# Experts in units of 32 rows in column groups, with whole fp32 weights in a ring, instead of blocks of 128 rows with split weights

## What is computed

```
lg   = v @ w_rg + b_rg                      # 4 groups of experts; the best group is taken
le   = v @ w_re + b_re                      # 8 experts in each group; the best 2 of the group
eid  = g_sel * 8 + top_i                    # 2 experts for each of 1032 rows: 2064 assignments
def expert_block(xb, e):                    # 32 experts, D = 1024, FF = 512
    hb = silu(xb @ w_gate[e]) * (xb @ w_up[e])     # 1024 -> 512, twice
    return hb @ w_down[e]                          # 512 -> 1024
f    = sum over the 2 experts of gate * expert_block(v)
y    = layer_norm(alpha * x1 + mod * f)
```

## Time and profile before

| | us |
|---|---|
| median of three runs | 1721.53 |
| the profiled execution | 1723.17 |
| its span, first to last instruction | 1721.5 |
| TensorE busy in the span | 1551.1 (90%) |
| VectorE, ScalarE, GpSimd busy | 1286.8, 798.7, 336.8 |
| moved by DMA | 365.95 MB, mean 213 GB/s |
| mean granted clock of TensorE | 0.947 of 2.4 GHz |

### The profile page before, as it was taken

One profiled execution on the slowest core, in us unless ns is written; L12 is line 12 of the kernel. 1 busy time (PEld: TensorE's weight loads), 2 busy tenths in 40 slices (PEclk: granted clock), 3 DMA queues, 4 the chain that ended last, 5 costly groups with the idle time before them and its releaser, 6 DMA issues.

```text
span 1721.5 us, 24475 instructions
## 1 busy us (share of the span) xinstructions
PE 1551.1 (90%) x8473; PEld 1310.2 (76%) x8473; DVE 1286.8 (75%) x1405; ACT 798.7 (46%) x689; POOL 336.8 (20%) x292
## 2 busy tenths in 40 slices
PE   5799999979999968999955899999999999999873
PEld 4788989978988956858844788888888888888630
DVE  5755647569998878767656778758978788699749
ACT  3322224255556655312220656457756565677510
POOL 4000002110000000000002233323434334344200
PEclk8999999989999988999965999999999999999986
DMA  9566227343333447332232769479978697899662
GB/s 295 189 227 234 65 78 236 123 140 120 105 112 126 136 158 244 110 99 88 65 145 103 303 235 376 175 304 364 376 281 324 246 376 273 331 353 369 266 241 109
DMA packets 135703, 365.95 MB, mean 213 GB/s; under 512 B 19120, under 2 KB 97968, under 8 KB 120152
## 3 DMA queue, kind: packets, MB, share of 16 engines
q1 hardware_dynamic: 113608, 308.19, 49.5%
q0 software_dynamic: 21456, 54.80, 9.1%
q10 hardware_dynamic: 576, 2.10, 0.4%
HBM read 333.07 MB, written 54.90 MB: 225 GB/s over the span
## 4 chain that ended last, share of the span: by engine, by line
PE 53%; DVE 4%; issue 2%; SPq 2%; DMA 1%; ACT 0%; POOL 0%; POOLq 0%; DVEq 0%; ACTq 0%
PE PS L2083 24%; PE PS L2116 13%; PE PS L1966 9%; PE PS L2076 2%; PE PS L2149 1%; PE PS L2105 1%; PE PS L1997 1%; PE PS L2032 1%; SPq L1597 1%; PE PS L1989 1%; DVE st L2489 0%; SPq L1602 0%; DVE lower L2480 0%; DVE arena L2497 0%; DVE arena L2485 0%
## 5 line engine op out<-in xcount | busy, mean ns | idle before, releaser
L2083 PE MATMUL PS<-big 128*128 128x512 f32 x1824 | 435.4, 395 | 8.4 <-DVE big L2425 5.1
L881 PE MATMUL PS<-big 128*128 128x352 f32 x2592 | 435.8, 328 | 1.6 <-DVE big L1135 1.6
L881 PEld LDWEIGHTS PS<-big 128*128 128x128 f32 x2592 | 424.4, 191 | 10.4 <-issue 6.7
L2083 PEld LDWEIGHTS PS<-big 128*128 128x128 f32 x1824 | 342.5, 190 | 81.6 <-issue 10.5
L2402 DVE TENSOR_TENSOR big<-lower,big 128x4096 fp32r<-128x4096 f32 x64 | 283.1, 4424 | 38.4 <-ACT big L1876 36.8
L1876 ACT ACTIVATE big<-lower 128x4096 fp32r<-128x4096 f32 x64 | 231.9, 3625 | 5.5 <-DMA lower<-in_w_gate_dram 3.6
L2116 PE MATMUL PS<-low,big 128*128 128x512 f32 x912 | 224.3, 401 | 9.3 <-DVE big L2444 9.3
L2116 PEld LDWEIGHTS PS<-low,big 128*128 128x128 f32 x912 | 170.0, 190 | 48.6 <-issue 9.6
L2402 DVE TENSOR_TENSOR low<-arena,low 128x4096 fp32r<-128x4096 f32 x32 | 141.6, 4425 | 63.3 <-ACT low L1876 63.2
L1739 POOL COPY scur<-idxS 128x1 int32 x38 | 115.6, 3042 | 258.5 <-ACT arena L1909 258.5
L1876 ACT ACTIVATE low<-arena 128x4096 fp32r<-128x4096 f32 x32 | 116.3, 3635 | 75.3 <-DMA arena<-in_w_down_dram 38.2
(11 more groups left out here) (410 smaller groups left out, 1996.3 us busy)
## 6 DMA issues: line engine op xcount, KB each, us to landing
lower<-in_w_gate_dram SPq DMA_DIRECT2D x32, 2048.0 KB, 9.0
lower<-in_w_up_dram SPq DMA_DIRECT2D x32, 2048.0 KB
arena<-in_w_down_dram SPq DMA_DIRECT2D x32, 2048.0 KB
arena<-in_w_ada_dram SPq DMA_DIRECT2D x16, 1024.0 KB, 6.6
arena<-in_w_in_dram SPq DMA_DIRECT2D x20, 512.0 KB, 8.0
upper<-in_w_ada_dram SPq DMA_DIRECT2D x8, 1024.0 KB, 11.7
upper<-in_w_in_dram SPq DMA_DIRECT2D x16, 512.0 KB, 3.8
arena<-acs_d SPq DMA_DIRECT2D x8, 1024.0 KB, 4.7
```

What stands on the lines that cost most here:

```text
L881: mm = pe.matmul(PS[:, 3 * b + a, 0:CH], wss[b][:, i, k, :], us[:, j, k, a * CH:(a + 1) * CH], start=(k == 0 and (i, j) == PARTS[0]), stop ...
L2083: mm = pe.matmul(PS[:, bank, :], xs[:, i, c, :], w[:, j, c, :], start=(c == 0 and (i, j) == PARTS[0]), stop=(c == KT - 1 and (i, j) == PAR ...
```

## The change

The unit of expert work becomes 32 rows (`CAP` = 32). A row of 1024 values is treated as four quarters of 256 (`QW` = 4, `DQ` = 256): one gather brings 32 tokens x 4 quarters = 128 pieces of 1 KB, piece q of token r to partition 32q + r. After 2 transposes `xT` has, for each quarter q and half c, a 128x32 block.

- **Matmuls in plain fp32.** No operand is split. The 32 columns of `xT` are the stationary operand, the weights are the moving one, and four matmuls stand side by side in the four column groups of the array (output partitions 0, 32, 64, 96): gate for c = 0 and 1, up for c = 0 and 1. The sum over the two halves is made by the turn: `h_turn` multiplies by `pick`, a 128x64 matrix of ones and zeros that adds pairs of groups, four matmuls. `down` puts four column ranges of 256 in the four groups.
- **Weights whole.** `ring` holds three experts of 128x12288 fp32: slot 0 is `wcur`, the expert being multiplied, two slots wait. Expert 0 is loaded straight to slot 0. For a new expert ScalarE copies gate (4 pieces of 128x1024), VectorE copies up (4 pieces) and down (one 128x4096) from the waiting slot to `wcur`. Each piece may be copied when the last unit of the expert before has used it.
- **Loads.** SyncE goes over the 32 experts in code written out. It sends the three first experts at `pb_mm`; then gate and up of x+2 once those of x are copied, and down of x+1 once that of x-1 is. Gate and up now have 4 KB in a row, down 16 KB.
- **Index columns.** VectorE copies them instead of GpSimd. `xg`, `yo`, `icur`, `scur` have two buffers.
- **Table.** It has 104 columns instead of 48, and is made by other small operations; a third little chain of 3 matmuls (`CTL_MM`) brings it to one partition. For each unit it holds whether the expert is new, which one it is and its slot.
- **Loop.** It runs over pairs of units. With the rows above there are 81 units (1 3 1 6 3 2 1 9 3 1 4 2 1 2 1 7 1 2 8 2 3 2 1 5 1 1 1 2 1 1 1 2 by expert), and an empty one makes the number even.
- After the loop, the buffers of the combining stage lie elsewhere; its instructions are the same.

The core of the diff (helpers `load_gate_up`, `gate_copy`, `up_copy`, `down_copy`, `gate_up` are new):

```
-CAP = 128
-NOV = 16
+CAP = 32
+NOV = 64
...
+        ring = sb("ring", [P, 9 * KT * FF], scope=ring_scope)
...
 # SyncE
+                def load_gate_up(x):
+                    s = SLOTS - x % SLOTS if x else 0
+                    for i, src in enumerate((w_gate, w_up)):
+                        sp.dma_start(ring[:, SLOT * s + 4096 * i:SLOT * s + 4096 * i + 4096]
+                                     .rearrange("p (q f) -> p q f", q=QW),
+                                     src[0, x].rearrange("(q p c) f -> p q (c f)", q=QW, p=P)).then_inc(we_loaded[s], 16)
...
+                for x in range(NE):
+                    sp.wait_ge(we_loaded[SLOTS - x % SLOTS if x else 0], 48 * ((x + 1) // SLOTS if x else 1))
+                    sp.sem_inc(we_here, 1)
+                    if x >= 2 and x + 1 < NE:
+                        sp.wait_ge(down_copied, copied_down(x - 1))
+                        load_down(x + 1)
+                    if x >= 1 and x + 2 < NE:
+                        chunks = copied_gate_up(x)
+                        sp.wait_ge(gate_copied, chunks)
+                        sp.wait_ge(up_copied, chunks)
+                        load_gate_up(x + 2)
...
 # ScalarE
+                def gate_copy(u, before):
+                    new = act.value_load(ctl[0:1, bass.ds(u, 1)], min_val=0, max_val=1)
                     with act.If(new > 0):
+                        here = act.value_load(ctl[0:1, bass.ds(u + NBLK, 1)], min_val=1, max_val=NE)
+                        w = act.value_load(ctl[0:1, bass.ds(u + 2 * NBLK, 1)], min_val=SLOT, max_val=SLOT * SLOTS)
+                        act.wait_ge(we_here, here)
+                        for q in range(QW):
+                            act.wait_ge(gu_mm, before * QW + (q + 1))
+                            act.activation(wcur[:, 1024 * q:1024 * q + 1024], ring[:, bass.ds(w + 1024 * q, 1024)],
+                                           ACT.Copy).then_inc(gate_copied, 1)
...
+                with act.Fori(1, pairs) as j:
+                    for b in range(2):
+                        half_tanh(j * 2 + b)
+                        gate_copy(j * 2 + (b + 2), j * 2 + (b + 1))
+                        hb_out(j * 2 + (b + 1))
+                        y_out(j * 2 + b, j, b)
...
 # TensorE
+                    for q in range(QW):
+                        pe.wait_ge(gate_copied, u * QW + (q + 1))
+                        pe.wait_ge(up_copied, u * QW + (q + 1))
+                        for g in range(4):
+                            part, c = g // 2, g % 2
+                            mm = pe.matmul(PS[32 * g:32 * g + 32, 3, :], xT[:, c, CAP * q:CAP * q + CAP],
+                                           wcur[:, 4096 * part + 1024 * q + 512 * c:4096 * part + 1024 * q + 512 * c + FF],
+                                           start=(q == 0), stop=(q == QW - 1))
...
 # VectorE
+                with ve.Fori(1, pairs) as j:
+                    for b in range(2):
+                        h_out(j * 2 + b)
+                        up_copy(j * 2 + (b + 2), j * 2 + (b + 1))
+                        x_out(j * 2 + (b + 2))
+                        gather_rows(j * 2 + (b + 4), b)
+                        scatter_rows(j * 2 + b, j, b)
+                        down_copy(j * 2 + (b + 1))
```

More of the change, by code:

```diff
@@ L1621, in _ @@
                 sp.wait_ge(vector_once, CTL_READY)
[L1622 to L1633, removed]
-                            sp.wait_ge(split, e + 1)
-                            load(dst, src, expert, rows, done)
-                        with sp.If(new < 1):
-                            sp.wait_ge(split, e + 1)
-                            sp.sem_inc(done, 16)
@@ new lines, in _ @@
+                gp.wait_ge(vector_once, IDXS_READY)
+                pairs = gp.value_load(ctl[0:1, CTL_N:CTL_N + 1], min_val=NE // 2 - 1, max_val=(NE + NOV) // 2 - 1)
+                for u in range(2):
+                    gather(u + 4, u)
+                    scatter(u, u)
+                with gp.Fori(1, pairs) as j:
+                    for b in range(2):
+                        gather(j * 2 + (b + 4), b)
+                        scatter(j * 2 + b, b)
+                for b in range(2):
+                    scatter(pairs * 2 + b, b)
@@ new lines, in _ @@
+                act.wait_ge(vector_once, CTL_READY)
+                pairs = act.value_load(ctl[0:1, CTL_N:CTL_N + 1], min_val=NE // 2 - 1, max_val=(NE + NOV) // 2 - 1)
+                act.wait_ge(we_here, 1)
+                act.sem_inc(gate_copied, QW)
+                gate_copy(1, 0)
+                hb_out(0)
+                for u in range(2):
+                    half_tanh(u)
+                    gate_copy(u + 2, u + 1)
+                    hb_out(u + 1)
+                    y_out(u, 0, u)
@@ L2064, in _ @@
                 mm.then_inc(tensor_once, 1)
+                pe.wait_ge(vector_once, UNIT_READY)
+                for i in range(3):
+                    mm = pe.matmul(PS[0:1, 5, P * i:P * i + P], unit_of[:, i:i + 1], ident[:, :], start=True, stop=True)
+                mm.then_inc(tensor_once, 1)
                 pe.wait_ge(gpsimd_once, PLACES_READY)
@@ L2133, in _ @@
-                gate(n_extra + (NE - 1))
-                h_turn(n_extra + (NE - 2))
-                up(n_extra + (NE - 1))
-                down(n_extra + (NE - 2))
-                h_turn(n_extra + (NE - 1))
-                down(n_extra + (NE - 1))
-                pe.wait_ge(yo_ready, n_extra + NE)
+                pairs = pe.value_load(ctl[0:1, CTL_N:CTL_N + 1], min_val=NE // 2 - 1, max_val=(NE + NOV) // 2 - 1)
+                x_turn(0, 0, 0)
+                gate_up(0)
+                x_turn(1, 0, 1)
@@ new lines, in _ @@
+                for u in range(2):
+                    h_turn(u)
+                    gate_up(u + 1)
+                    x_turn(u + 2, 1, u)
+                    down(u)
+                with pe.Fori(1, pairs) as j:
+                    for b in range(2):
+                        h_turn(j * 2 + b)
+                        gate_up(j * 2 + (b + 1))
+                        x_turn(j * 2 + (b + 2), j + 1, b)
+                        down(j * 2 + b)
+                h_turn(pairs * 2)
+                gate_up(pairs * 2 + 1)
@@ L2141, in f_sum @@
+                down(pairs * 2)
+                h_turn(pairs * 2 + 1)
+                down(pairs * 2 + 1)
+                pe.wait_ge(yo_ready, pairs * 2 + 2)
                 def f_sum(t, rows):
@@ L2473, in _ @@
+                h_out(pairs * 2)
+                scatter_rows(pairs * 2, pairs, 0)
+                down_copy(pairs * 2 + 1)
+                h_out(pairs * 2 + 1)
+                scatter_rows(pairs * 2 + 1, pairs, 1)
                 ve.wait_ge(rows2n_loaded, 48)
```

583 lines of the change are left out of this document (267 added, 316 removed).

## The result

The changed kernel takes 1732.15 us (median of 15 runs, 1725.76 to 1739.02), the kernel before in the same runs 1721.93 (1719.58 to 1727.17). The ratio is 1.0053, with a 95% interval of 1.0038 to 1.0067: slower, by about half a per cent. The forecast was 1679 and faster. The profiled span is 1734.5 us (before 1721.5).

The account below looks back on a forecast made before the run. TensorE's matmuls were taken to bound the 702.9 us expert loop. First gate at 937, loop 665 (units 558, new experts 50, waits 55, ends 2) and tail 77.1 - 1.4 made 1677.7, forecast 1679 us; range 1640 to 1750.

Parts of the forecast that it names:

- A unit on TensorE: Expert loop, one unit: matmul rounds, turns and changes of shape sum to 6.56 us, taken as 6.8 with hand-overs.
- the "7.1" end of the unit: Expert loop: the upper end for a unit, 7.1 us, with 0.93 and 0.49 us for the rounds.
- my recurrence: Expert start times from 6.8 us a unit, 1.6 a new expert and 17 us between weight arrivals; loop 665 us.
- my own case: The forecast itself for the whole kernel: 1679 us, its own range 1655 to 1710, chance 0.60.
- A new expert: At 31 expert changes TensorE stalls 1.6 us (ends 0 and 3), waiting for ScalarE's reads, copies and `hb_out`.
- The supply: Weight loads in the expert loop: 17 us between arrivals where behind; waits for weights of 55 us in all.
- Before the loop: Making the routing table: gate starts near 937 us instead of 941.6, 4.6 us less.
- After the loop: Combining stage: a narrower last output copy and an index copy already done, 1.4 us less.
- rival 2: VectorE's expert copies run at one element a cycle: stall about 3.2 us, supply interval 20, time 1738 us; chance 0.10.
- rival 3: Expert loop: short reads and free switches hide stalls, unit 6.5 us, loop 604, time 1618 us; chance 0.10.
- Rival 1: Expert loop: late scatters hold VectorE at `scatter_rows`; units of 8 us give 1759 us; chance 0.17.
- Rival 4: Expert loop: the four column groups don't overlap, a unit costs 22 us, loop 1804, 2820 in all; chance 0.03.

Follow-up runs that it names:

- e1: Changed kernel with `hb` written so that `h_turn` reads its stationary without a step: 1657.4 us, ratio 0.9616 to the kernel before.
- e5: e4 with only the first half of each expert's down weights loaded from expert 3 on (outputs wrong): 1622.92 us, one run.
- e4: Changed kernel with the edits of e1 and e3 together: 1651.59 us, ratio 0.9583 to the kernel before.
- e6: Changed kernel with `h_turn` reading every third value of `hb` (12 bytes apart, output wrong): 1695.02 us, one run.
- e2: As e1, but `h_turn`'s stationary is read with a step of 2 values (8 bytes): 1655.97 us, one run.
- e3: Changed kernel with ScalarE's `hb_out` put ahead of the gate copies at a new expert, step kept: 1703.85 us, ratio 0.9885 to the kernel before.

## Why the prediction was wrong

**The step that failed** is the third term of "A unit on TensorE": "`h_turn`: 4 fp32 matmuls with few columns; eight take 1.71 us, so 0.86". I took the price from rows with a stationary of the same type and size, and didn't look at how it lies in memory. It measured 2.01. For a load without a step give a fair price (e1: 1.03); the step adds 0.98. The Trainium skill has the rule, which I did not weigh (Advanced Engine Details and Errata, SBUF Cachelines): SBUF is read in lines of 16 bytes, and full speed needs at least two hits in a line. The four runs agree: with no step and with one of 8 bytes a line serves four and two values, at 192 and 196 ns; 12 and 16 bytes leave fewer than two, at 263 and 329 ns. The other page on it (SBUF — State Buffer, Door 1: The DMA port swizzle) reads it as a stride of four fp32 values for free, which the measurement contradicts for this load. The transposes fit neither reading well: their load is 202 ns at 8 bytes, where a line still serves two values, against 140 without a step.

The kernel before has no plain fp32 matmul with a step in a load of this size, so no row gave the price. It had the sign told above, 204 ns against 140, on the same `hb`. So the term wanted two ends, and I gave it none: the "7.1" end of the unit has other causes. 1.15 us in 82 units are 94 us; my recurrence, fed with 7.95 in place of 6.8 and nothing else, gives about 742 for the loop, 1756 in all. The sign of the result hangs on this one term, and with it mended (e1) the time is 1657, inside the range I gave for my own case.

The measured loop is 66 us longer than the 665 forecast: 88 more in 81 units of 7.89, 24 less in waits and clock (81 against 105), 2 more at the ends. Two errors in opposite directions made the miss smaller than the failed term alone would have.

**The rest of the unit** was forecast at 5.7 with 0.24 of hand-overs and measured 5.88. Gate and up came at 3.57 (3.41 and two changes of shape at 0.08), down at 1.86 (1.71 and two changes). The 0.15 read from the earlier trace rows fits. The Trainium skill names a drain at a change of tiling mode (TensorEngine Tiling, Tiling Modes); the rows show a small cost of about 0.08 us a change, and no run shows what makes it. `x_turn` was too short by 0.17. The hand-overs that I added as 0.24 don't exist inside an expert; that they made the sum nearly right is luck.

**A new expert** was the right mechanism in the right place: reads of 0.63 us each (forecast 0.7), copies of 1.0 (1.06), then `hb_out`, which TensorE waits for. The wait was 0.77 us rather than 1.6, as TensorE came back to `h_turn` 0.3 us later (5.88) and ScalarE was done 0.5 us sooner (`hb_out` ends 6.7 us after the gate's start, forecast 7.2). What I didn't have is the clock: in ten cases the wait is followed by matmuls at half clock, which cost 1.4 to 1.7 us. Of the copies on VectorE, the one of 1024 took 0.69 us and the one of 4096 2.30 (forecast 0.81 and 3.2). The Trainium skill (VectorE: DVE Perf Modes, Mode 2×_2P) would have 0.53 for the first; the measurement lies between the rule and my row. The two copies differ by 1.61 us for 3072 values, which is the pace of the rule; what it leaves out is 0.15 us in each copy.

**The supply** was forecast at 17 us an expert and is 15.7, which e5 shows to be bytes over rate. Its 15.6 for the weights, from the rates of the earlier trace rows, was right; the small pieces took 0.4 us rather than 1.1 (2.7% of the engines' time in the 46.9 us of e4's three steps), and I had rounded the sum up.

**Before the loop** I had 937 and it is 927.5. The second chain of 36 matmuls takes 4.26 us, where I let it run at half clock as its predecessor in the earlier trace rows did:

```profile
914.38 7.44 PE L2064 MATMUL PS<-arena 128*128 128x104 f32 x36 [14.33 <-DVE arena L2374]
921.75 0.81 PE L2068 MATMUL PS<-ident,unit_of 128*1 128x128 f32 x6
922.50 4.26 PE L2072 MATMUL PS<-arena 128*128 128x104 f32 x36
...
927.51 3.64 PE L2091 MATMUL PS<-ring,arena 128*32 128x512 f32 x32 [0.52 <-DVE arena L2408]
```

The three chains now follow one another without a gap, and the second has the full clock (1.00 in 922.5:926.7, against 0.50 in 927:935 of before). The first begins 4 us before my 918.3: the shorter list of masks gave 5 us, not 1. After the loop 77.1 - 1.4 = 75.7 was forecast and 76.1 came.

**Slips in the sums**, none of which moves the forecast: by the earlier trace rows the tail of before is 77.0 us and not 77.1. The recurrence as it is written gives 716 for rival 2 and 615 for rival 3, where 724 and 604 stand. The parts of the chances add up to 0.72 faster, 0.06 same and 0.22 slower.

**The rivals.** Rival 1 gave a time near the result (unit of 8 us: 1759) by the wrong mechanism: nothing waits at L2424. VectorE is never idle ahead of its 82 scatter copies, as here at the same expert, and gathers land in at most 7.4 us:

```profile
1324.49 0.14 DVE L2424 COPY scur<-lower 128x1 int32 x1
```

A unit over 7.4 us was to be read as this rival, and would have been read wrongly: the length alone named no cause, the row of L2100 did. Rival 2 is out by the copies on VectorE (mean in ns):

```profile
L2441 DVE COPY ring<-ring 128x1024 f32 x124 | 78.0, 689 | 101.3 <-PE PS L2091 52.0
...
L2451 DVE COPY ring<-ring 128x4096 f32 x31 | 71.1, 2295 | 53.9 <-PE PS L2110 27.9
```

Rival 3 (no stalls, 15.6 us an expert, unit 6.5) is half of what e4 shows: the waits for `hb_out` do go once the order is changed, but the unit is 6.91, and the waits for weights stay. Rival 4 is out by the first row of the unit above: 32 records in 3.57 us, as four groups side by side.

## What to carry to other kernels

Price a weight load by how its values lie and by what kind of matmul it serves, not by shape and type alone. The row with the same index expression was the old transpose (204 ns), the row with the same kind of matmul had no step (192), and the load that has both took 329. Where the trace has no load that agrees in both, give the term two ends. A step in the stationary can be moved into the copy that writes it, where here it cost nothing. On an in-order engine, put what TensorE waits for ahead of copies that are only needed a phase later; a wait of 0.8 us was followed by up to 1.7 us of lost clock, in ten places.

## What was not expected of the hardware

- The load of a 128 x 128 stationary for a plain fp32 matmul takes 192 ns from neighbouring values, 196 with a step of 8 bytes, 263 with 12 and 329 with 16. For a transpose of fp32 values it takes 140, and 202, 204 and 192 with steps of 8, 16 and 32 bytes. ScalarE read the same step from PSUM and wrote without one at no cost (0.60 us for 128x512).
- Of TensorE's 28 waits for `hb_out` six were at late weights (5.2 us or more), each followed by a gate and up that ran partly at half clock. Of the other 22, most of 0.7 to 1.0 us, ten were (0.51 in 2.7 us). With `h_turn` at 1.54 us (e6) two were; with it at 1.04 and 1.09 (e1, e2), and in e3, which has these waits no more, none before expert 14. What decides it was not tried.
- Weight loads (rows of 4 KB, and 16 KB for down) ran at 403 GB/s with DMA at 1.00 for 95 us on end, and at 410 with 1.02 for 47 us in e4, while 1 KB gathers and scatters went beside them and landed in 7.4 us at most.
- A VectorE copy in SBUF of 128x4096 fp32 took 2.30 us, which is 1.8 values a nanosecond in each partition; ScalarE's takes 1.0 us for 1024.
